# Identity products ahead of four waits of TensorE: at three stage ends and at the first gate item

## The chip, the cores and the metric

The kernel runs on one core of one Trainium2 chip. A core has five engines that run their own streams of instructions and meet at semaphores: TensorE (in the rows PE; its weight loads are PEld), VectorE (DVE), ScalarE (ACT), GpSimd (POOL) and SyncE (SP), which issues most of the DMAs. TensorE reads operands from SBUF and writes psum, eight banks of 2 KB per partition, 512 columns of fp32 each. TensorE's clock has two levels, 1.2 and 2.4 GHz; the profile shows the granted share of the full one as PEclk, 0.50 and 1.00. The metric is the device time of one execution in microseconds.

## The reference

Two transformer blocks, one after the other, on a sequence of 1024 tokens of width 1024, batch 1, in fp32. The first mixes a sliding-window attention (window 128, 8 heads, with sinks) and an mLSTM; the second mixes a retention and a sparse attention that picks, for each query, the highest-scored keys by an indexer. Each has a feed-forward part.

```python
def first_block(x, c, ...):
    shift_m, scale_m, gate_m, shift_f, scale_f, gate_f = jnp.split(c @ w_ada + b_ada, 6, axis=-1)
    h = modulate(rms_norm(x, g_pre_mix), shift_m, scale_m)
    q_a, k_a, v_a, q_m, k_m, v_m, o_m, i_m, f_m, g_a, g_m = jnp.split(h @ w_in, ...)
    # window attention y_a; conv, silu, mlstm_chunkwise, head_layer_norm -> y_m
    # sigmoid(g_a) * (y_a @ w_branch_attn) + sigmoid(g_m) * (y_m @ w_branch_mlstm), then @ w_out
    # x + gate * rms_norm(...); then gate/up/down feed-forward, x + gate * rms_norm(...)

def second_block(x, ...):
    rq, rk, rv, rg, aq, ak, av, iq, ik, iw = split_columns(rms_norm_2(h, mix_norm_pre) @ w_in)
    ret_out = retention(rope(rq), rope(rk), rv, rg)
    att_out = dsa_attention(rope(aq), rope(ak), av, rope(iq), rope(ik), iw)   # top-k keys per query
    h = h + rms_norm_2(concatenate([ret_out, att_out]) @ w_out, mix_norm_post)
    up = causal_dwconv(rms_norm_2(h, ffn_norm_pre) @ w_up, conv_w, conv_b)
    h = h + rms_norm_2((silu(g) * u) @ w_down, ffn_norm_post)

reference = second_block(first_block(x, ...), ...)
```

## The kernel before

Every large product is made in three parts to reach fp32's precision on a faster format: an operand x is split into a high part (rounded, made mostly by ACT) and a low part (the rest, made by POOL or DVE), and `multiply` (L132 to L136) issues high x high (L134), low x high (L135) and high x low (L136), 512 columns each.

The program is a row of stages, each a `with nc.Block()`, in which each engine has its own hand-written order: rows of the first block, window attention with the convolution, the recurrent stage, then (`scores_phase`) the output projection, the feed-forward part of the first block and the index scores of the second, then the spread stage (`spread_phase`), then (`close_last`) the second block's output projection and feed-forward part. A stage ends with a barrier of all five engines: each engine drains (a DRAIN on its queue) and signals, POOL collects the signals and releases all. Between the stages of this change `core.renew_sems` (L83 to L87) then clears the semaphores (POOL) and makes a second such barrier.

`recurrent_phase` (L1018): the mLSTM in chunks of 128 tokens, beside it 16 gate products; at its end TensorE runs, for 16 items i, `gate(M + i, 0, KD)` and `branches(i)`, the last of which VectorE merges into `mT` (L1338 to L1341). The next stage begins with `Closing.pe` (L2158), whose first products (L2136) wait for the first operand split by ACT (L2066) and DVE (L2075); its first weights, `w_hi`/`w_lo` or `next_hi`/`next_lo`, lie ready.

`scores_phase` (L2461) ends on TensorE with `unit(n)` (L2575): products of keys and index queries, which ACT passes through relu (L2790) and DVE adds up into `bias` (L2704), eight units to a tile of queries.

`spread_phase` (L3310): 40 items (c, t), five groups of 512 columns of `w_in_2` (Q_, K_, V_, G_ gates, A_ attention queries) by eight tiles of 128 tokens; the bank of an item is `bank(n)`, n % 3 up to the gates. The weights of a group come k by k: SP loads `raw`, ACT makes the high part (L3692), POOL the low one (L3651); the first two k of Q_ (`first_hi`, `first_lo`) lie ready. VectorE runs a bitwise search for the top-k threshold (L2926 to L2951) throughout, with the rope of an item (L3580 to L3583) or a step of the retention between its steps; ACT counts for it (L2940) and copies V_ items out of psum (L3749). `bank_free(n)` lets TensorE wait until the item three before has been read. At the first gate item (G_, 0), TensorE waits for the banks of items n and n + 1, turns the first keys (`ret.turn_keys`, L3016 to L3019) and then computes both items in turns (`pair`). The stage ends with the last values of the sparse attention (L3201), the transposes of the sums (L3220), and VectorE's last scaling.

`Closing.keep_warm` (L2182) is there before: products of the identity with itself, 128 columns into a bank that nobody reads. It is called with 6 at L2178 and with 5 at L1635, in the output projection of each block.

Of the kernel before, what the change touches and what calls it, by code (L numbers as in the profile page):

```python
# [13 lines left out]
P = 128  # L14
# [117 lines left out]
def multiply(nc, out, stationary, moving, start, stop):  # L132

    nc.tensor.matmul(out, stationary.hi, moving.hi, start=start, stop=False)  # L134
    nc.tensor.matmul(out, stationary.hi, moving.lo, start=False, stop=False)  # L135
    return nc.tensor.matmul(out, stationary.lo, moving.hi, start=False, stop=stop)  # L136
# [881 lines left out]
def recurrent_phase(core, at, h, wv, wba, wbm, qT, kT, v, R, gcol, dec, yaT, soT, w_norm, ya, ym, mT, spill, next_w, cst):  # L1018
# [31 lines left out]
    INTER, UPDATE, INTRA = (5, 6), (7, 4), (3, 2)  # L1050
    head_at = lambda banks, hd: core.ps[:, banks[hd // 2], hd % 2 * E:(hd % 2 + 1) * E]

    with nc.Block() as block:
# [80 lines left out]
        def _(pe):  # L1134
            def gate(s, first, last):
                T, hf = s // 2, s % 2
                if first == 0:
                    if hf == 0 and T:
                        pe.wait_ge(split_done, T)
                    if s >= 2:  # L1140
                        pe.wait_ge(sig_done, s - 1)
                for k in range(first, last):
                    done = multiply(nc, core.ps[:, hf, :], w[:, T % 2, k], h.half(k, hf), k == 0, k == KD - 1)
                if last == KD:
                    done.then_inc(mm_done, 1)
# [51 lines left out]
            def branches(i):  # L1197
                m, hf = i // 2, i % 2
                tok = slice(hf * HALF, (hf + 1) * HALF)
                if i == 0:  # L1200
                    pe.wait_ge(ya_lo, KB)
                    pe.wait_ge(ym_lo, KB)
                if hf == 0:
                    pe.wait_ge(wb_split, m + 1)
                if i >= 2:
                    pe.wait_ge(merged, i - 1)
                for b, y in enumerate((ya, ym)):
                    for k in range(KB):
                        last = multiply(nc, core.ps[:, 2 + 2 * hf + b, :], wb[:, b, k], y(k, tok), k == 0, k == KB - 1)
                last.then_inc(br_done, 1)  # L1210

            for st in range(STEPS):
                n = at_step(st, 0, EVERY, TB)
                if n is not None:
                    opening(n)
                n = at_step(st, EVERY // 2, EVERY, TB)
# [6 lines left out]
            for i in range(M):  # L1223
                gate(M + i, 0, KD)
                branches(i)

        @block.vector
        def _(dve):
# [732 lines left out]
        return 3 if conv else 2  # L1961


class Closing:


# [42 lines left out]
    def at_step(self, u):  # L2009

        return (u, u % 2 * 2) if u < self.kt else ((u - self.kt) % self.kt, (u - self.kt) % 4)
# [168 lines left out]
                self.turn(pe, 2 * (u - kt - 10) + 1)  # L2180

    def keep_warm(self, bank, many):  # L2182
        for _ in range(many):
            self.nc.tensor.matmul(self.core.ps[:, bank, 0:P], self.cst["ident"], self.cst["ident"], start=True, stop=True)

    def turn_bank(self, n):
        return 4 + n % 2 if n < KD else self.late_banks[n % len(self.late_banks)]
# [273 lines left out]
def scores_phase(core, stage, closing, h, wv, base, tables, tables_dram, cos, sin, cst, k_hi, k_lo, av, iw, bias, first_raw, first_w):  # L2461
# [23 lines left out]
    bank = lambda n: (0, 2, 1)[n % 3]  # L2485
# [16 lines left out]
    with nc.Block() as block:  # L2502
# [26 lines left out]
        def _(pe):  # L2529
# [21 lines left out]
            def left(what):  # L2551

                if what[0] == S_:
                    pe.wait_ge(keys_out, what[1] + 1)
                else:
                    pe.wait_ge(parts_out_done, parts_no[what] + 1)

            def turn(c, t, a=0):
                m = place[c, t, a]
                if m < 3:  # L2560
                    pe.wait_ge(closing.squared, closing.square_no(15))
                else:
                    left(turns[m - 3 if m < 12 else m - 1])
                at = turn_bank(m)
                if c == S_:
                    pe.wait_ge(rr_ready, number[c, t] + 1)
                    for j in range(2):
                        last = nc.tensor.transpose(core.ps[:, at, j * P:(j + 1) * P], rs[:, t % 2, j * P:(j + 1) * P], cst["ident"])
                else:
                    pe.wait_ge(q_lo, t - 1)  # L2570
                    for q in range(4):
                        last = nc.tensor.transpose(core.ps[:, at, q * P:(q + 1) * P], q_rows[:, 4 * a + q, :, :].bitcast(F32), cst["ident"])
                last.then_inc(turned, 1)
# [73 lines left out]
            for n in range(3 * RH, len(units)):  # L2647
                unit(n)
                if n - 3 * RH in (4, 7):
                    turn(I_, 7, (n - 3 * RH) // 6)  # L2650

        @block.vector
        def _(dve):
# [656 lines left out]
def spread_phase(core, h, wv, cos, sin, cst, bias, retention_of, spill, q_rows, q_tiles, tops, sparse_of, first_w, next_w, next_raw, next_first):  # L3310
# [12 lines left out]
    with ExitStack() as scope:  # L3323
# [6 lines left out]
        bank = lambda n: n % 3 if n < A_ * TB else n % 2  # L3330
# [41 lines left out]
        with nc.Block() as block:  # L3372
# [34 lines left out]
            def _(pe):  # L3407
# [58 lines left out]
                def turn_free(what):  # L3466
                    if place[what]:
                        pe.wait_ge(turn_out, place[what])
# [14 lines left out]
                for n, (c, t) in enumerate(items):  # L3483
                    if c == Q_ or t > 1 or (c, t) == (A_, 0):
                        bank_free(n)
                    elif t == 0:
                        bank_free(n)
                        if c == G_:
                            bank_free(n + 1)
                    if c == G_ and t == 0:  # L3490
                        turn_free((K_, 0))
                        ret.turn_keys(pe, 0).then_inc(turned, 1)
                        pair(n, 0, 4)
# [65 lines left out]
                for half in range(2):  # L3559
                    att.values(pe, TB * RH - 2, half)  # L3560
                att.turn_sums(pe, TB - 1)

            @block.vector
            def _(dve):
# [434 lines left out]
```

## Time and profile before

| | |
|---|---|
| time, median of 3 runs | 2876.22 us (2875.53 to 2876.64) |
| the profiled execution: its time | 2871.56 us |
| its span, first to last instruction | 2869.8 us |
| mean granted TensorE clock over the span | 0.984 |
| TensorE busy | 2753.2 us, 96%, 13656 products |
| VectorE busy | 1806.6 us, 63% |
| ACT, POOL busy | 1244.5 us, 43%; 1177.1 us, 41% |
| DMA | 272.35 MB, mean 95 GB/s |

A wait's releaser is the instruction whose semaphore came last. A product's row starts when it starts to stream; its duration holds the latency through the array, so that the rows of one stream overlap, and the distance of two starts is what one costs. Most large products run as one instruction each in the trace; a view of the trace counts instructions, the order counts products as the program issues them. A DRAIN stands on the engine's queue ("PEldq", "DVEq"); its start is when the queue reaches it and its duration how long it holds there.

### The profile page before, as it was taken

How to read it: one execution, taken by the hardware profiler on the slowest of the kernel's cores; microseconds unless marked ns; L12 is line 12 of the kernel's file. 1: busy time of each engine (PE TensorE's matmuls, PEld its weight loads, DVE VectorE, ACT ScalarE, POOL GpSimd, SP SyncE). 2: the span in 40 equal slices, each digit the busy share in tenths (PEclk: the TensorE clock that was granted, in tenths of full speed). 3: DMA queues.
4: the chain of work that ended last, by engine and by line, in shares of the span. 5: the costliest groups of instructions: out<-in, count | busy, mean ns of one | idle time of the engine just before them, and what ended most of it. 6: DMA issues, size and time to landing. Idle time of an engine off the chain costs nothing. (4 is left out here: it accounts for less than half of the span.)

```text
span 2869.8 us, 38822 instructions
## 1 busy us (share of the span) xinstructions
PE 2753.2 (96%) x13656; PEld 2260.2 (79%) x13656; DVE 1806.6 (63%) x2690; ACT 1244.5 (43%) x2267; POOL 1177.1 (41%) x826
## 2 busy tenths in 40 slices
PE   6999999999999999999999899989999999999998
PEld 6877788887788888888888677877778888887886
DVE  6758757323676666621845999785567778776153
ACT  6225545101533333323654677547453444443243
POOL 2011222333734444544641242521173466675454
PEclk8999999999999999999999999999999999999999
DMA  7431112323422222245530123100242222124452
GB/s 261 154 118 30 30 45 63 107 66 103 140 78 70 88 88 74 87 169 164 180 119 2 44 67 96 46 15 9 82 147 67 81 73 88 66 80 169 151 192 90
DMA packets 176237, 272.35 MB, mean 95 GB/s; under 512 B 13145, under 2 KB 105561, under 8 KB 176089
## 3 DMA queue, kind: packets, MB, share of 16 engines
q1 hardware_dynamic: 176088, 270.39, 28.6%
q8 instruction: 91, 1.49, 0.2%
q14 instruction: 58, 0.47, 0.1%
HBM read 224.21 MB, written 46.14 MB: 94 GB/s over the span
## 5 line engine op out<-in xcount | busy, mean ns | idle before, releaser
L2083 POOL TENSOR_TENSOR sb_out_lo<-sb_out_raw,sb_out_hi 128x512 fp32r<-128x512 f32 (+1 forms) x174 | 311.9, 1801 | 312.2 <-ACT sb_out_hi L2070 312.1
L134 PE MATMUL psum<-sb_out_hi,sb_a_hi 128*128 128x512 f32 x912 | 357.8, 392 | 5.7 <-ACT sb_junk L2294 4.4
L136 PE MATMUL psum<-sb_out_hi,sb_a_lo 128*128 128x512 f32 x912 | 355.1, 389 | 0.0
L135 PE MATMUL psum<-sb_out_lo,sb_a_hi 128*128 128x512 f32 x912 | 355.0, 389 | 0.0
L1556 POOL TENSOR_TENSOR sb_pair_lo<-sb_pair_sum,sb_pair_hi 128x512 fp32r<-128x512 f32 x180 | 236.7, 1326 | 269.7 <-ACT sb_pair_hi L1700 269.7
L134 PE MATMUL psum<-sb_h_hi,sb_w_hi 128*128 128x512 f32 x640 | 256.7, 401 | 2.9 <-DVE sb_h_lo L2230 2.4
L136 PE MATMUL psum<-sb_h_hi,sb_w_lo 128*128 128x512 f32 x640 | 249.6, 390 | 0.0
L135 PE MATMUL psum<-sb_h_lo,sb_w_hi 128*128 128x512 f32 x640 | 249.6, 390 | 0.0
L134 PE MATMUL psum<-sb_h_hi,sb_pair_hi 128*128 128x512 f32 x576 | 224.1, 389 | 0.0
L135 PE MATMUL psum<-sb_h_lo,sb_pair_hi 128*128 128x512 f32 x576 | 224.1, 389 | 0.0
L136 PE MATMUL psum<-sb_h_hi,sb_pair_lo 128*128 128x512 f32 x576 | 224.1, 389 | 0.0
L1700 ACT ACTIVATE sb_pair_hi<-sb_pair_sum 128x512 fp32r<-128x512 f32 x180 | 113.2, 630 | 237.6 <-DVE sb_pair_sum L1840 164.2
L134 PE MATMUL psum<-sb_w_hi,sb_h_hi 128*128 128x512 f32 (+1 forms) x496 | 197.4, 398 | 12.0 <-DVEq L3583 5.0
L134 PEld LDWEIGHTS psum<-sb_out_hi,sb_a_hi 128*128 128x128 f32 x912 | 171.2, 188 | 46.4 <-ACT sb_junk L2294 7.3
L136 PEld LDWEIGHTS psum<-sb_out_hi,sb_a_lo 128*128 128x128 f32 x912 | 171.2, 188 | 36.0
L135 PEld LDWEIGHTS psum<-sb_out_lo,sb_a_hi 128*128 128x128 f32 x912 | 171.3, 188 | 34.3
L1909 DVE TENSOR_TENSOR sb_gate_up<-sb_gate_up,psum 128x512 f32<-128x512 f32 x216 | 138.6, 682 | 86.0 <-PE psum L136 84.1
L136 PE MATMUL psum<-sb_w_hi,sb_h_lo 128*128 128x512 f32 (+1 forms) x496 | 190.7, 384 | 0.0
L135 PE MATMUL psum<-sb_w_lo,sb_h_hi 128*128 128x512 f32 (+1 forms) x496 | 190.6, 384 | 0.0
L134 PE MATMUL psum<-sb_h_sum_hi,sb_pair_hi 128*128 128x512 f32 x432 | 168.4, 390 | 1.8 <-ACT sb_gate_up L1760 1.2
L1840 DVE TENSOR_TENSOR sb_pair_sum<-sb_pairs_raw 128x512 f32<-128x512 f32 x144 | 161.8, 1144 | 10.6 <-POOL sb_pair_lo L1556 8.2
L135 PE MATMUL psum<-sb_h_sum_lo,sb_pair_hi 128*128 128x512 f32 x432 | 168.1, 389 | 0.0
(487 smaller groups left out, 6383.9 us busy)
## 6 DMA issues: line engine op xcount, KB each, us to landing
act_kept<-sb_gate_up SPq DMA_DIRECT2D x40, 512.0 KB, 2.8
sb_pairs_raw<-in_w_up SPq DMA_DIRECT2D x18, 1024.0 KB, 5.2
sb_late_w<-in_w_ada SPq DMA_DIRECT2D x32, 512.0 KB, 4.8
sb_w_raw<-in_w_in SPq DMA_DIRECT2D x54, 256.0 KB, 3.1
sb_out_raw<-in_w_ffn_down SPq DMA_DIRECT2D x44, 256.0 KB, 3.1
sb_out_raw<-in_w_down SPq DMA_DIRECT2D x44, 256.0 KB, 2.8
sb_act_ring<-act_kept SPq DMA_DIRECT2D x40, 256.0 KB, 4.0
sb_act_late<-act_kept SPq DMA_DIRECT2D x40, 256.0 KB, 4.0
```

The source lines that it names most:

```text
L134: nc.tensor.matmul(out, stationary.hi, moving.hi, start=start, stop=False)
L135: nc.tensor.matmul(out, stationary.hi, moving.lo, start=False, stop=False)
L136: return nc.tensor.matmul(out, stationary.lo, moving.hi, start=False, stop=stop)
L1556: self.nc.gpsimd.tensor_tensor(self.wp.lo[:, p], src, self.wp.hi[:, p].bitcast(F32), ALU.subtract).then_inc(self.pair_lo, 1)
L1700: self.nc.scalar.activation(self.wp.hi[:, p], src, ACT.Copy).then_inc(self.pair_hi, 1)
L1840: ops.tensor_tensor(t, a, b, op).then_inc(self.pair_sum if p < self.by_dve else self.pool_pair, 1)
L1909: nc.vector.tensor_tensor(dest, a, self.core.ps[:, bank, :], op).then_inc(self.part, 1)
L2083: self.nc.gpsimd.tensor_tensor(w.lo, raw, w.hi.bitcast(F32), ALU.subtract).then_inc(self.w_lo, 1)
```

## The change

A function `keep_warm(core, cst, pe, bank, many)` issues `many` products of the identity with itself, 128 columns each, into one bank; the method of `Closing` calls it now. Four calls are new. In `recurrent_phase` 36 products into bank 5 stand at the end of TensorE's program (site 1). In `scores_phase` 54 into bank 3 stand at its end (site 2). In `spread_phase` 22 into `bank(n)` stand at the first gate item behind its `bank_free` calls and ahead of `turn_free` (site 3), and 26 into bank 4 at the end (site 4). No other engine's instructions change.

```diff
@@ -1223,6 +1223,7 @@
             for i in range(M):
                 gate(M + i, 0, KD)
                 branches(i)
+            keep_warm(core, cst, pe, INTER[1], 36)
 
         @block.vector
         def _(dve):
@@ -1961,6 +1962,11 @@
         return 3 if conv else 2
 
 
+def keep_warm(core, cst, pe, bank, many):
+    for _ in range(many):
+        pe.matmul(core.ps[:, bank, 0:P], cst["ident"], cst["ident"], start=True, stop=True)
+
+
 class Closing:
 
 
@@ -2180,8 +2186,7 @@
                 self.turn(pe, 2 * (u - kt - 10) + 1)
 
     def keep_warm(self, bank, many):
-        for _ in range(many):
-            self.nc.tensor.matmul(self.core.ps[:, bank, 0:P], self.cst["ident"], self.cst["ident"], start=True, stop=True)
+        keep_warm(self.core, self.cst, self.nc.tensor, bank, many)
 
     def turn_bank(self, n):
         return 4 + n % 2 if n < KD else self.late_banks[n % len(self.late_banks)]
@@ -2648,6 +2653,7 @@
                 unit(n)
                 if n - 3 * RH in (4, 7):
                     turn(I_, 7, (n - 3 * RH) // 6)
+            keep_warm(core, cst, pe, 3, 54)
 
         @block.vector
         def _(dve):
@@ -3488,6 +3494,7 @@
                         if c == G_:
                             bank_free(n + 1)
                     if c == G_ and t == 0:
+                        keep_warm(core, cst, pe, bank(n), 22)
                         turn_free((K_, 0))
                         ret.turn_keys(pe, 0).then_inc(turned, 1)
                         pair(n, 0, 4)
@@ -3559,6 +3566,7 @@
                 for half in range(2):
                     att.values(pe, TB * RH - 2, half)
                 att.turn_sums(pe, TB - 1)
+                keep_warm(core, cst, pe, 4, 26)
 
             @block.vector
             def _(dve):
```

TensorE at the end of the recurrent stage, before: the last products of `branches` (`sb_ym` is the mLSTM's output, `sb_branch` the branch weight), the branch out of the block and into the next, the first products of the output projection. "waits" names the semaphores waited for; names are shared by semaphores of other stages.

```order
L136 MATMUL psum<-sb_ym_hi_3903,sb_branch_lo_3913 128x512
L134 MATMUL psum<-sb_ym_hi_3903,sb_branch_hi_3912 128x512
L135 MATMUL psum<-sb_ym_lo_3904,sb_branch_hi_3912 128x512
L136 MATMUL psum<-sb_ym_hi_3903,sb_branch_lo_3913 128x512
L1053 UNCONDITIONAL_BRANCH
L2528 UNCONDITIONAL_BRANCH [waits barrier_Pool_Activation_PE_DVE_SP_release]
L134 MATMUL psum<-sb_w_hi_82,sb_a_hi_6607 128x512 [waits y_ready_61,root_60]
```

The same place in the changed program:

```order
L136 MATMUL psum<-sb_ym_hi_3903,sb_branch_lo_3913 128x512
L134 MATMUL psum<-sb_ym_hi_3903,sb_branch_hi_3912 128x512
L135 MATMUL psum<-sb_ym_lo_3904,sb_branch_hi_3912 128x512
L136 MATMUL psum<-sb_ym_hi_3903,sb_branch_lo_3913 128x512
L1967 MATMUL psum<-sb_consts_49 128x128 x36
L1053 UNCONDITIONAL_BRANCH
L2533 UNCONDITIONAL_BRANCH [waits barrier_Pool_Activation_PE_DVE_SP_release]
L134 MATMUL psum<-sb_w_hi_82,sb_a_hi_6643 128x512 [waits y_ready_61,root_60]
```

The 36 products stand ahead of the branch with the barrier, behind all real work of the stage. Sites 2 and 4 read alike, with 54 and 26.

TensorE at the first gate item, before: the last products of the V_ group, the transposes of the first keys (L3019), the first gate product. `raw_got5_99` is the name under which the wait for ACT's reading of the bank appears.

```order
L134 MATMUL psum<-sb_w_hi_13493,sb_h_hi_14_62 128x512
L135 MATMUL psum<-sb_w_lo_13494,sb_h_hi_14_62 128x512
L136 MATMUL psum<-sb_w_hi_13493,sb_h_lo_15_63 128x512
L3019 MATMUL psum<-sb_consts_49,sb_k_rows_13463 128x128 [waits hi_done_102,x_got5_41,raw_got5_99]
L3019 MATMUL psum<-sb_consts_49,sb_k_rows_13463 128x128 x3
L134 MATMUL psum<-sb_w_hi_13493,sb_h_hi_12_60 128x512 [waits raw_got1_95]
L135 MATMUL psum<-sb_w_lo_13494,sb_h_hi_12_60 128x512
```

The same place in the changed program, where the transposes' line is L3025:

```order
L134 MATMUL psum<-sb_w_hi_13583,sb_h_hi_14_62 128x512
L135 MATMUL psum<-sb_w_lo_13584,sb_h_hi_14_62 128x512
L136 MATMUL psum<-sb_w_hi_13583,sb_h_lo_15_63 128x512
L1967 MATMUL psum<-sb_consts_49 128x128 [waits raw_got5_99]
L1967 MATMUL psum<-sb_consts_49 128x128 x21
L3025 MATMUL psum<-sb_consts_49,sb_k_rows_13553 128x128 [waits x_got5_41,hi_done_102]
L3025 MATMUL psum<-sb_consts_49,sb_k_rows_13553 128x128 x3
L134 MATMUL psum<-sb_w_hi_13583,sb_h_hi_12_60 128x512 [waits raw_got1_95]
```

The wait for ACT's reading moved from the transposes to the first identity product.

For the counts, the old call with 6 products in the program before (`sb_consts` holds the identity), among the products of the output projection and the transposes of L2196:

```order
L134 MATMUL psum<-sb_out_hi_6605,sb_a_hi_6607 128x512
L135 MATMUL psum<-sb_out_lo_6606,sb_a_hi_6607 128x512
L136 MATMUL psum<-sb_out_hi_6605,sb_a_lo_6608 128x512
L2184 MATMUL psum<-sb_consts_49 128x128 x6
L2196 MATMUL psum<-sb_consts_49,sb_rows_mid_6603 128x128 [waits late_got0_76]
L2196 MATMUL psum<-sb_consts_49,sb_rows_mid_6603 128x128 x7
L134 MATMUL psum<-sb_out_hi_6605,sb_a_hi_6607 128x512 [waits y_ready_61,root_60]
```

Nothing moves here; in the profile this line has 44 instructions for the two calls of each block, 6 and 5 products.

## Rows read from the trace of the kernel before

**Rows 1.** all waits of TensorE: line, releaser, us in total, times, longest
```profile
PE psum L134 <- DVE sb_a_lo L2075: 10.0, 3, 5.2
PE psum L134 <- POOLq L3654: 7.7, 1, 7.7
```

**Rows 2.** windows: length, busy us and counts by engine, PEclk, DMA share, GB/s
```profile
46.30:49.20 2.90, 2.82 (x13) 2.52 (x12) 2.21 (x6) 2.08 (x4) 0.00 (x0) 0.50 0.98 372
...
692.90:699.60 6.70, 4.11 (x10) 3.28 (x11) 2.86 (x10) 2.72 (x4) 0.78 (x1) 0.50 0.68 212
...
1616.00:1766.00 150.00, 142.86 (x608) 113.44 (x608) 140.04 (x377) 108.30 (x214) 49.94 (x38) 0.97 0.25 78
...
1768.10:1774.80 6.70, 5.13 (x14) 3.89 (x15) 6.60 (x8) 5.55 (x11) 5.27 (x4) 0.50 0.37 89
...
1788.60:1795.30 6.70, 6.70 (x40) 6.47 (x38) 4.74 (x14) 1.70 (x4) 1.75 (x2) 0.50 0.09 28
...
2061.70:2064.90 3.20, 3.20 (x9) 2.46 (x8) 1.63 (x7) 1.58 (x2) 0.61 (x1) 0.50 1.07 346
```

**Rows 3.** timeline of TensorE, site 1: start, us, instruction, [idle before <-releaser]
```profile
689.95 0.39 PE L136 MATMUL psum<-sb_ym_hi,sb_branch_lo 128*128 128x512 f32 x1
695.49 0.80 PE L134 MATMUL psum<-sb_w_hi,sb_a_hi 128*128 128x512 f32 x1 [5.15 <-DVE sb_a_lo L2075]
...
697.36 0.63 PE L135 MATMUL psum<-sb_w_lo,sb_a_hi 128*128 128x512 f32 x1
697.78 0.63 PE L136 MATMUL psum<-sb_w_hi,sb_a_lo 128*128 128x512 f32 x1
...
699.81 0.39 PE L135 MATMUL psum<-sb_w_lo,sb_a_hi 128*128 128x512 f32 x1
700.04 0.39 PE L136 MATMUL psum<-sb_w_hi,sb_a_lo 128*128 128x512 f32 x1
```

**Rows 4.** line of the barrier ending the recurrent stage: took min/median/max ns, start
```profile
L1053 PEldq DRAIN  x1: 4267/4267/4267, 686.1 to 686.1; - x1
L1053 DVEq DRAIN  x1: 725/725/725, 691.8 to 691.8; - x1
```

**Rows 5.** timeline of TensorE: groups of 128-column products
```profile
46.21 2.91 PE L239 MATMUL psum<-sb_consts 128*128 128x128 f32 x12
...
776.52 1.50 PE L2184 MATMUL psum<-sb_consts 128*128 128x128 f32 x12
...
2186.72 1.28 PE L2184 MATMUL psum<-sb_consts 128*128 128x128 f32 x10
```

**Rows 6.** line of the barrier that ends the spread stage
```profile
L3372 DVEq DRAIN  x1: 698/698/698, 2058.0 to 2058.0; - x1
```

**Rows 7.** timeline of TensorE, site 4
```profile
2056.62 0.66 PE L3220 MATMUL psum<-sb_consts,sb_inverse_sums 128*128 128x128 f32 x4
2061.22 0.50 PE L134 MATMUL psum<-sb_next_hi,sb_a_hi 128*128 128x512 f32 x1 [3.95 <-DVE sb_a_lo L2075]
```

**Rows 8.** line of the barrier that ends the scores stage
```profile
L2502 DVEq DRAIN  x1: 17/17/17, 1614.0 to 1614.0; - x1
```

**Rows 9.** timelines of TensorE and POOL, site 2 and the stage behind it
```profile
1607.60 0.39 PE L2587 MATMUL psum<-sb_ik_lo,sb_iq_tile 128*128 128x512 f32 x1
...
1621.18 0.52 PE L134 MATMUL psum<-sb_w_hi,sb_h_hi 128*128 128x512 f32 x1
...
1619.83 7.54 POOL L3651 TENSOR_TENSOR sb_w_lo<-sb_w_raw,sb_w_hi 128x512 fp32r<-128x512 f32 x6 [31.20 <-ACT sb_w_hi L3692]
...
1720.10 0.69 PE L134 MATMUL psum<-sb_w_hi,sb_h_hi 128*128 128x512 f32 x1 [3.05 <-DVEq L3583]
```

**Rows 10.** timeline of TensorE, site 3 and the next meeting with VectorE
```profile
1768.65 1.09 PE L3019 MATMUL psum<-sb_consts,sb_k_rows 128*128 128x128 f32 x4 [3.72 <-ACT sb_rotated L3749]
1770.76 0.80 PE L134 MATMUL psum<-sb_w_hi,sb_h_hi 128*128 128x512 f32 x1 [1.02 <-POOL sb_w_lo L3651]
...
1788.28 0.60 PE L3044 MATMUL psum<-sb_state,sb_q_decayed 128*128 128x128 f32 x2 [1.90 <-DVE sb_scores L3098]
```

## The prediction

> **What bounds the kernel now.** I read the page first: TensorE (PE in the rows) is busy 96% of a span of 2869.8 us. What is left to win on it are 117 us of idle time and the stretches in which its products ran slowly. Then I read the list of its waits, sorted by length, and the timelines around the longest. Four are the places of this change: 5.2 us at the end of the recurrent stage (site 1), 7.7 us at the end of the scores stage (site 2), 3.7 us at the first gate item (site 3) and 3.95 us at the end of the spread stage (site 4) [rows 1, 7, 10]. Behind sites 1, 3 and 4 TensorE resumes at 1.2 GHz: the windows show a granted clock of 0.50 [rows 2]. At that level 512 columns cost 0.43 us, at 2.4 GHz 0.23 us [rows 3]. After site 1 ten products run so, 10 x 0.20 = 2.0 us lost; after site 4 a little over 3.2 us do, half of it lost, 1.7 us [rows 2].
>
> Then I asked who ends each wait. Sites 1, 2 and 4 are ends of a stage, and a stage ends with a barrier of all engines. The view of the barrier's line shows a DRAIN on each engine's queue. TensorE's at site 1 starts at 686.1 and holds for 4.27 us, until 690.37, right when its last product ends (689.95 + 0.39) [rows 3, 4]. So a DRAIN waits for the products ahead of it. VectorE's ends last, at 691.8 + 0.73 = 692.53 [rows 4]. TensorE's slack at site 1 is therefore 692.53 - 690.37 = 2.2 us, not 5.15. The other 695.49 - 692.53 = 2.96 us lie behind the DRAINs (the release, a second barrier, ACT's and VectorE's split of the first operand), and no work ahead of the barrier can lie beside them.
>
> **What an added product costs.** The call exists already with 6 products and with 5, as the order shows. The timeline has them as 12 and as 10 instructions: an fp32 product that is no transpose runs as two. They take 1.50 and 1.28 us, so one more product costs 0.22 us [rows 5]. That makes 1.50 + 30 x 0.22 = 8.1 us for 36, 12.1 us for 54, 5.0 us for 22 and 5.9 us for 26, all at full clock. This step carries the whole forecast: reading the rows as one instruction per product gives half. At half clock the nearest row is six such products at 46.21: 2.91 us, 0.485 us each, at a clock of 0.50 [rows 2, 5].
>
> *The Trainium skill ("TensorE: Matmul & The Clock Gate", section "Back-to-back issue gap") gives some 81 ns for each product of 128 columns in a stream. By that 36 would take 2.9 us and 26 would take 2.1 us, the DRAINs of sites 1 and 4 would end some 0.6 and 0.5 us behind VectorE's and that of site 2 before it, a sum of about +1. The page's figure is not for fp32; the rows are of this very call, read 0.22 us, and decide.*
>
> **Site 1, 36 products.** They start one slot behind the last real one, at 690.18, and end at 698.3. TensorE's DRAIN then ends 698.3 - 692.53 = 5.8 us behind VectorE's. All engines wait for it, and so do the loads of the next stage, which are issued behind the barrier: **+5.8 us**, with nothing to hide it.
>
> **Site 2, 54 products.** From one slot behind the last real product, 1607.83, until 1619.9. VectorE's DRAIN, the last one, ended at 1614.0 + 0.02 [rows 8, 9]. **+5.9 us**. VectorE's top-k search, which fills the next stage, starts that much later: it is busy 140.04 of the first 150 us there [rows 2] and cannot catch up.
>
> **Site 4, 26 products.** The four transposes before them start at 2056.62 and take four slots of 0.11 us, so they run from 2057.06 until 2063.0; VectorE's DRAIN ended at 2058.0 + 0.70 = 2058.70 [rows 6, 7]. **+4.3 us**.
>
> **What the clock gives back.** Behind the barriers TensorE idles as before: 2.96 us at site 1, 2061.22 - 2058.70 = 2.52 us at site 4, 1.7 us at site 2 (1607.60 + 0.39 + 7.7 = 1615.7, less 1614.02) [rows 1, 8, 9]. In this trace the clock fell around a wait of 3.05 us (the product at 1720.10 reads 0.69 us, one behind a wait at full clock 0.52) and around one of 1.90 us that had small products before it (0.50 for the 6.7 us behind 1788.6) [rows 2, 9, 10]. The new idle times lie between, with dense work ahead of them. I take half of what there is to win: -1.0 of 2.0 us at site 1, **-0.8** of 1.7 at site 4, with bounds of nothing and all. At site 2 a full clock buys nothing: the first twelve products use weights that lie ready, the next need one that loads, ACT and POOL make behind the barrier. POOL makes six in 7.54 us from 1619.83, the first by 1621.1, and TensorE, at half clock, takes it at 1621.18 [rows 9]. Twelve faster products only lengthen that wait by 2.4 us.
>
> **Site 3, 22 products.** The order shows that they don't stand where the words say. The long wait (3.72 us, ended by ACT's copy L3749) is for a free bank; the products stand behind it, so that wait is now on the first of them, and they run when the real work is ready. Before, four transposes at 1768.65 took 1.09 us and TensorE then idled 1.02 us for POOL's first weight [rows 10]. That is the cover. The clock was at half from 1768.1 on [rows 2]; with dense products I let half clock last some 3.4 us, as behind 2061.7, so 5.0 us of products become 6.7. The first gate product comes 6.7 - 1.0 = 5.7 us late less 0.5 for faster transposes; its nine slow successors [rows 2] are then fast, 1.8 us. That is 3.4 us late. The next meeting with VectorE is at 1788.28, where TensorE waited 1.90 us [rows 10]: 1.5 us are left. With no such wait the clock may hold behind it, which spares up to half of 6.7 us. Bounds: -2 us if it does, and 22 x 0.485 - 1.0 - 1.9 = +7.8 us if all run at half clock. I take **+1.0**, near the row of 2061.7.
>
> **Sum.** 5.8 + 5.9 + 4.3 - 1.0 - 0.8 + 1.0 = **+15.2 us** on the profiled execution of 2871.56 us. It was 4.66 us faster than the median of the three timed runs; the terms are barriers that every run has, so they are added to the median: 2876.22 + 15.2 = **2891.4 us**, +0.53%. What lies within 0.2%, 5.75 us (2870.5 to 2882.0), counts as the same, since a measurement of this kernel can tell about that much from no change.
>
> **The rivals.**
> - *The forecast*, 0.56: 2891.4, by itself 2888.5 to 2894.5.
> - *B, the clock holds everywhere*, 0.18: dense identity products keep it at 2.4 GHz over all the idle times. 16.0 - 2.0 - 1.7 and site 3 at -2 to +1: +10.3 to +13.3, 2888. *The Trainium skill's rule ("TensorE: Matmul & The Clock Gate", "Why this matters for your kernels") is to leave no long idle gaps between bursts, so that the rate doesn't drop; by that rule B comes.* Against it stands the fall around 1.90 us.
> - *E, the gate item at half clock*, 0.14: the 22 products never get the full clock, and the delay reaches ACT's copy of the turned keys and so VectorE: 16.0 - 1.8 + 7.8 = +22: 2898.2.
> - *C, no slower: TensorE's DRAIN doesn't hold the others*, 0.06: they pass the barrier at their old times and only TensorE is late. It is 698.3 - 695.49 = 2.8 us late at site 1 and 1.8 at site 4, less the clock's 2.0 and 1.7; at site 2 it comes at 1619.9, its twelve products end 1.5 us behind POOL's weight, which VectorE's search hides. With site 3 that is +1.9: 2878.1, the same. Against it: the DRAIN's end at 690.37.
> - *D, one instruction per product in this build*, 0.04: 4.1, 6.1, 2.6 and 3.0 us. Sites 1 and 4 move by 1.8 and 1.4, site 2 by nothing, less 1.8 for the clock: +1.4, 2877.6; with all of the clock and of site 3, 2870, faster. It needs half of the rows' counts.
> - *F, the clock falls within the identity products*, 0.02: 2905.
>
> Range: D and C left out below, F above: 2887.0 to 2899.0. Chances: slower 0.90; same 0.09 (C, most of D); faster 0.01.
>
> **What would show it.** 72, 108, 44 and 52 instructions on the new line, 0.11 us apart. TensorE's DRAIN is the last at the three barriers, 5.8, 5.9 and 4.3 us behind VectorE's; the first product follows 2.96, 1.70 and 2.52 us behind it. If the clock behind sites 1 and 4 reads 1.00, B is right; if VectorE's DRAIN is still the last and the others pass, C. At site 3 the first identity product starts with the end of ACT's copy. The forecast is wrong if the three DRAINs are not late by 16 us together, or if the spread stage from barrier to barrier grows by other than 4.3 us and -2 to +3.

## The result, and the profile after

The changed kernel takes 2885.62 us (median of 7 runs, 2883.26 to 2886.55), the kernel before in the same comparison 2875.53 us (7 runs, 2871.66 to 2876.74). The ratio is 1.0038, with an interval of 1.0027 to 1.0050: **10.1 us slower**. The sign of the forecast and its largest part, the late barriers, are right; the time lies below its range (2887.0 to 2899.0) and 5.8 us below the forecast. A later comparison of the same two kernels (below, e11_after) gave 1.0043 (1.0029 to 1.0057), and all runs of this study together have medians of 2873.35 us before (111 runs, 2863.34 to 2880.21) and 2885.3 us after (14 runs): +12.0 us.

The profiled execution of the changed kernel has a span of 2883.8 us and 13932 products on TensorE where the one of before has 13656: 276 more, two for each of the 138 added. The first view is the lines of the three barriers (minimum/median/maximum ns, start), VectorE's and TensorE's DRAIN of each; they answer to [rows 4, 6, 8].

```profile
L1053 DVEq DRAIN  x1: 725/725/725, 695.6 to 695.6; - x1
L1053 PEldq DRAIN  x1: 2173/2173/2173, 700.1 to 700.1; - x1
...
L2507 DVEq DRAIN  x1: 17/17/17, 1619.2 to 1619.2; - x1
L2507 PEldq DRAIN  x1: 2173/2173/2173, 1623.0 to 1623.0; - x1
...
L3378 DVEq DRAIN  x1: 698/698/698, 2068.0 to 2068.0; - x1
L3378 PEldq DRAIN  x1: 2173/2173/2173, 2070.9 to 2070.9; - x1
```

TensorE's DRAIN now ends last each time: at 702.27 against VectorE's 696.33, at 1625.17 against 1619.22, at 2073.07 against 2068.70. That is 5.9, 6.0 and 4.4 us, 16.3 together; the forecast had 5.8, 5.9 and 4.3.

The waits of TensorE (line, releaser, us in total, times, longest) show the other side, to be read against [rows 1]:

```profile
PE psum L134 <- DVE sb_a_lo L2081: 6.4, 3, 3.0
...
PE psum L1967 <- ACT sb_rotated L3757: 3.8, 1, 3.8
```

The idle time at site 1 is 3.0 instead of 5.2 us. The one at site 3 is as long as before and now ends on the first identity product: the products stand behind it. In the list the kernel looks better than before, and it is slower: what left this list went into the DRAINs, which the list doesn't show.

Windows of the changed kernel (length, busy us and counts of PE, PEld, DVE, ACT and POOL, PEclk, DMA share, GB/s), at the places of [rows 2]:

```profile
705.80:709.20 3.40, 3.40 (x9) 2.64 (x8) 1.53 (x6) 1.58 (x2) 0.53 (x1) 0.50 1.06 345
2075.50:2078.70 3.20, 3.15 (x14) 2.60 (x15) 2.17 (x9) 1.01 (x2) 0.00 (x0) 1.00 1.03 330
1787.00:1793.80 6.80, 6.80 (x42) 5.35 (x41) 6.63 (x11) 5.86 (x12) 5.44 (x4) 1.00 0.60 185
```

Behind site 1 the clock was at half for 3.4 us; before it had been so for 6.8 us, of which 4.2 lay behind the first product (695.49 to 699.7). Behind site 4 it held; behind the gate item it was full. The barriers' 16.3 us stand against a span that grew by 14.0 us, but the two traced executions differ by 3.8 us ahead of site 1 already, where the programs are the same. One pair of traces therefore doesn't tell where the rest went. The experiments give the stages of 18 executions.

### The profile page after: what moved, and what is told of

Same layout as the page of the kernel before. It is cut to its first block and busy times, and to the rows that moved or that the text cites. A ratio compares the mean times of both kernels' runs of the same rounds, so it can differ in the third digit from the quotient of the medians.

```text
span 2883.8 us, 39374 instructions
## 1 busy us (share of the span) xinstructions
PE 2779.0 (96%) x13932; PEld 2286.8 (79%) x13932; DVE 1804.0 (63%) x2690; ACT 1244.6 (43%) x2267; POOL 1178.9 (41%) x826
## 5 line engine op out<-in xcount | busy, mean ns | idle before, releaser
L134 PE MATMUL psum<-sb_w_hi,sb_h_hi 128*128 128x512 f32 (+1 forms) x496 | 196.9, 397 | 12.9 <-DVEq L3591 5.0
```

## The experiments

Each stage is measured from the end of the last DRAIN of one barrier to the end of VectorE's DRAIN at the next; "late" is how far the last DRAIN ends behind VectorE's. All in us, one traced execution a row. The expectations end the last stage at VectorE's last DRAIN instead, 3.0 us earlier (808.1 us for the 811.1 of the first row).

| execution | start to site 1 | late | site 1 to 2 | late | site 2 to 4 | late | site 4 to the end | span |
|---|---|---|---|---|---|---|---|---|
| before | 692.5 | 0 | 921.5 | 0 | 444.7 | 0 | 811.1 | 2869.8 |
| before (e0) | 695.4 | 0 | 918.4 | 0 | 442.4 | 0 | 810.5 | 2866.7 |
| before (e12) | 691.7 | 0 | 918.5 | 0 | 446.0 | 0 | 810.6 | 2866.8 |
| before (e13) | 696.6 | 0 | 920.3 | 0 | 449.3 | 0 | 812.2 | 2878.4 |
| after | 696.3 | 5.9 | 916.9 | 6.0 | 443.5 | 4.4 | 810.7 | 2883.8 |
| after (e11) | 695.2 | 5.8 | 916.7 | 6.0 | 443.3 | 4.4 | 812.5 | 2884.0 |
| after (e14) | 693.5 | 5.8 | 915.6 | 5.9 | 445.1 | 4.4 | 811.7 | 2882.1 |
| after (e15) | 696.0 | 5.9 | 915.6 | 6.0 | 443.1 | 4.4 | 812.1 | 2883.2 |
| e1, site 1 alone | 692.5 | 5.9 | 915.9 | 0 | 441.9 | 0 | 811.0 | 2867.3 |
| e2, site 2 alone | 694.0 | 0 | 917.9 | 6.0 | 443.0 | 0 | 811.6 | 2872.5 |
| e3, site 3 alone | 695.1 | 0 | 918.6 | 0 | 443.0 | 0 | 812.0 | 2868.7 |
| e4, site 4 alone | 694.1 | 0 | 917.8 | 0 | 445.2 | 4.4 | 809.5 | 2871.0 |
| e5, behind the barriers | 695.0 | 0 | 919.3 | 0 | 441.9 | 0 | 810.2 | 2866.4 |
| e6, within the slack | 697.4 | 0 | 920.5 | 0 | 445.8 | 0 | 810.5 | 2874.2 |
| e7, ahead and behind | 694.1 | 0 | 916.4 | 0 | 441.8 | 0 | 809.2 | 2861.5 |
| e8, 72 at site 1 | 696.4 | 13.9 | 919.6 | 6.0 | 446.2 | 4.4 | 808.9 | 2895.5 |
| e9, e7 with site 3 | 697.9 | 0 | 917.0 | 0 | 445.4 | 0 | 808.4 | 2868.7 |
| e10, e9 with 26 at site 2 | 695.2 | 0 | 918.0 | 0.3 | 443.5 | 0 | 809.8 | 2866.8 |

The late columns repeat within 0.1 us. Everything else moves by several us between executions of one kernel.

**One place at a time.** Of the four new calls three are left out; e1 keeps the first, e2 the second, e3 the third, e4 the last:

```diff
+            keep_warm(core, cst, pe, INTER[1], 36)
+            keep_warm(core, cst, pe, 3, 54)
+                        keep_warm(core, cst, pe, bank(n), 22)
+                keep_warm(core, cst, pe, 4, 26)
```

> Only the 36 products ahead of the barrier behind the recurrent stage; the other three places as before. Theory A (each place costs what its DRAIN comes late, and the clock gives back only what runs at half rate right behind it): TensorE's DRAIN at that barrier ends 5.8 to 5.9 us behind VectorE's, the stretch from that barrier to the one behind the scores stage is 0 to 2 us shorter, the whole is +4 to +6 us. Rival B (the products change the clock far behind the barrier as well, which gives the 4.6 us that the next stage was shorter in the changed kernel): the same 5.9 us at the barrier, but the stretch behind it is 4 to 5 us shorter, the whole +1 to +2 us. Rival N (the 4.6 us are chance: half-rate stretches that come and go in code the change doesn't touch): the stretch behind it differs from before's by -5 to +1 us in a way that kernels without these products show as well.

> Only the 54 products ahead of the barrier behind the scores stage. Theory A: TensorE's DRAIN ends 5.9 us behind VectorE's, the spread stage keeps its length within 0.5 us, the whole is +5.9 us. Rival B: the clock holds at the start of the spread stage and the stage is 1 us or more shorter, +4.9 us or less. Rival N: the time ahead of this barrier differs from before's by several us, though nothing there is changed.

> Only the 22 products at the first gate item. Theory A (as forecast): the spread stage from barrier to barrier is 1.0 us longer, with bounds of -2 and +7.8, the whole +1 us. Rival B: by the difference of the two traces (the spread stage was 1.15 us shorter with sites 2 and 3 together, from release to VectorE's DRAIN) these products win 1.2 us, the whole -1.2 us. Rival N: what lies ahead of the stage moves the whole by more than this.

> Only the 26 products ahead of the barrier behind the spread stage. Theory A: TensorE's DRAIN ends 4.3 to 4.4 us behind VectorE's; behind it half of 1.7 us is won, +3.5 us. Rival B: the clock reads 1.00 from the first product behind the barrier on, all of 1.7 us is won, +2.6 us. The changed kernel's trace had the clock at 1.00 there, but its last stages were only 0.4 us shorter, so A and B differ by what else moves there.

| kept | median us (before 2872.22) | ratio | interval | in us | forecast |
|---|---|---|---|---|---|
| site 1 | 2875.42 | 1.0012 | 1.0003 to 1.0021 | +3.4 | +4.8 |
| site 2 | 2879.36 | 1.0024 | 1.0015 to 1.0033 | +6.9 | +5.9 |
| site 3 | 2870.53 | 0.9998 | 0.9989 to 1.0007 | -0.6 | +1.0 |
| site 4 | 2875.80 | 1.0006 | 0.9997 to 1.0016 | +1.7 | +3.5 |

The column in us is the ratio times 2872; the medians themselves differ by +3.2, +7.1, -1.7 and +3.6 us, and each interval reaches some 2.6 us to either side. The four ratios add up to +11.4 us, 1.0040, and the change as a whole gave 1.0038 and 1.0043: within this noise the places add up. Site 1's +3.4 lies between theory A (+4 to +6) and B (+1 to +2), site 2's fits A, and sites 3 and 4 don't tell A from B. In e1 the clock never fell behind site 1 (the same columns of windows):

```profile
701.40:708.20 6.80, 6.76 (x38) 5.88 (x39) 2.70 (x10) 1.97 (x3) 3.34 (x2) 1.00 0.93 300
```

The stage behind it was short, 915.9 us, as rival B had it. But e2, e3 and e4, which have nothing at site 1, took 917.8 to 918.6 us and not the 921.5 of the first trace: a part of what looked like a gain was that trace. So N holds for a part of it, and how much is left for B one execution of e1 can't tell.

**Products where nobody waits for them.** e5 has none of the four calls and six products as the first work of the stages behind sites 1 and 4; e6 has only as many products as end before VectorE's DRAIN; e7 joins the two without site 2; e0 is the kernel before once more.

```diff
 class Closing:
     def pe(self, pe):
         kt, nc = self.kt, self.nc
+        if not self.before:
+            self.keep_warm(0, 6)
...
+            keep_warm(core, cst, pe, INTER[1], 9)
...
+                keep_warm(core, cst, pe, 4, 6)
```

e5 is the first hunk, e6 the other two and 26 products at site 2, e7 all that is shown.

> None of the four places. Instead six identity products behind the barriers of sites 1 and 4, as the first work of TensorE in the next stage (bank 0, which the stage's first product writes anew). Six take 1.3 us at full clock; the barrier's release came some 1.5 us behind the last DRAIN and the first product 2.96 us behind it, so they should end before its operand is there. Theory A (the clock is all that identity products can win, and they cost only where a DRAIN waits for them): no barrier later, the stage behind site 1 up to 2.0 us shorter than the 917.8 to 918.6 us that it took in the kernels without products there, the last stage up to 1.7 us shorter than 808.1 to 809.0; the whole -1 to -3.5 us. Rival B (the products must stand ahead of the idle time to hold the clock): both stages as before, the whole within 0.5 us of before.

> Products ahead of the barriers only as many as end before VectorE's DRAIN: 9 at site 1 (2.0 us in a slack of 2.15), 26 at site 2 (5.7 in 5.9), 6 at site 4 (1.3 in 1.34 to 1.44), none at site 3. Theory A: VectorE's DRAIN stays the last or TensorE's is late by 0.2 us at most, so the cost of +16.3 us is gone. What the clock gives depends on the idle time that is left, 3.0, 2.0 and 2.5 us as in the changed kernel: where it held there it holds here, -1.6 us behind site 1 and -1.0 behind site 4, the whole -3 us, 0.9990. Rival B (it takes the long run of products to hold the clock): 0 to -1 us.

> 9 products ahead of the barrier of site 1 and 6 ahead of that of site 4, and six behind each; sites 2 and 3 without. Theory A: no barrier late, TensorE never idle for more than some 2 us around either, clock 1.00 behind both, -2.0 and -1.7 us, the whole -3 to -3.7 us. Rival B (the clock falls all the same, or the six behind the barrier run at half clock, 0.485 us each, and delay the first product by 1.5 us): 0 to +3 us.

> The kernel before once more, for the length of its stages in a second traced execution. Theory N (4 us and more of the difference between the two traced executions came from code that the change doesn't touch): the stage between sites 1 and 2 takes 917.8 to 918.6 us, as in the three kernels without products at site 1, not the 921.5 of the first trace, and the way to site 1 692.5 to 694.5. Rival: 921.5 again, then the three others were shortened by something in them.

Measured, against a median of 2873.90 us of before: e5 2868.93 us, 0.9989 (0.9980 to 0.9998); e6 2872.78 us, 0.9996 (0.9987 to 1.0004); e7 2864.73 us, **0.9974 (0.9965 to 0.9983)**; e0 0.9999 (0.9990 to 1.0009). e5 gained what theory A allowed. e6 did not reach A's -3 us: the clock fell behind both of its barriers. e0 took 918.4 us between sites 1 and 2, as theory N said.

The timeline of TensorE in e5, where the six stand behind 3.76 us of idle time, and that of e7, where nine more stand ahead of it (start, us, instruction, [idle before <-releaser]):

```profile
696.63 2.58 PE L1966 MATMUL psum<-sb_consts 128*128 128x128 f32 x12 [3.76 <-PEq L86]
698.87 0.77 PE L134 MATMUL psum<-sb_w_hi,sb_a_hi 128*128 128x512 f32 x1
```

```profile
691.79 2.17 PE L1967 MATMUL psum<-sb_consts 128*128 128x128 f32 x18
695.71 1.57 PE L1967 MATMUL psum<-sb_consts 128*128 128x128 f32 x12 [1.75 <-PEq L86]
697.09 0.50 PE L134 MATMUL psum<-sb_w_hi,sb_a_hi 128*128 128x512 f32 x1
```

In e5 the clock has fallen, the six take 2.58 us instead of some 1.5, and the first real product comes 3.85 us behind the barrier instead of 2.97: behind a long idle time they are late themselves. (At site 4 of e5 the six stand behind 2.56 us of idle time; there they took 1.58 us and the clock held.) In e7 the idle time is cut into pieces of less than 2 us, the six run at full clock, and the first real product comes 2.97 us behind the barrier, as before. The windows of e7 behind sites 1 and 4 read full clock from the first product on:

```profile
697.10:703.90 6.80, 6.80 (x40) 5.96 (x39) 2.74 (x10) 2.64 (x3) 3.53 (x3) 1.00 1.00 298
2054.70:2058.00 3.30, 3.30 (x17) 2.77 (x16) 2.15 (x9) 1.30 (x2) 0.16 (x1) 1.00 1.02 328
```

Its barriers aren't late (TensorE's DRAIN at 691.8 + 2.17, VectorE's at 693.4 + 0.72). The gain, 7.5 us by the ratio and 4.9 at the interval's near end, is larger than the 3.7 us that theory A could pay for. Part of the rest has rows. The old identity products behind each barrier ([rows 5], 776.52 and 2186.72) serve as marks; in e7 they are at 776.17 and 2178.63:

```profile
776.17 1.50 PE L1967 MATMUL psum<-sb_consts 128*128 128x128 f32 x12
2178.63 1.28 PE L1967 MATMUL psum<-sb_consts 128*128 128x128 f32 x10
```

That is 82.05 and 126.3 us behind the barriers; the seven executions with nothing at site 1, and the seven with nothing at site 4, took 84.5 and 128.5 us on average. So 2.5 and 2.2 us, 4.7 together, lie right behind the two barriers. The stretch near 1502 us that e7 lacks (below) is worth 1.0 to 3.3 us where it comes; what is left has no row. The two DRAINs of e7 at site 1:

```profile
L1053 PEldq DRAIN  x1: 2168/2168/2168, 691.8 to 691.8; - x1
L1053 DVEq DRAIN  x1: 723/723/723, 693.4 to 693.4; - x1
```

**More and fewer.** e8 is the changed kernel with 72 for 36 at site 1. e9 is e7 with site 3's call, e10 is e9 with `keep_warm(core, cst, pe, 3, 26)` at site 2. e11 is the changed kernel again.

> The changed kernel with 72 products instead of 36 at site 1. Theory A (each product holds the barrier 0.22 us, one for one): TensorE's DRAIN ends 5.95 + 36 x 0.22 = 13.9 us behind VectorE's, the whole is 7.9 us slower than the changed kernel, 1.0038 + 0.0028 = 1.0066 of before. Rival C (a late DRAIN is partly made up for behind the barrier): less than 1.0055.

> The changed kernel once more, timed and traced beside the others. The four places alone gave 1.0012, 1.0024, 0.9998 and 1.0006, a sum of +0.40%: theory A (the places add up) expects 1.0040 within 0.001, the DRAINs late by 5.9, 5.9 and 4.4 us again, 916 to 917 us between sites 1 and 2 and 806.5 to 807.8 in the last stage. Rival N (the first comparison, +10.1 us, was low because its executions fell well): 1.0050 or more.

> 9 and 6 products ahead of the barriers of sites 1 and 4, six behind each, and the 22 at the gate item; none at site 2. Theory A (site 3 is worth -1.5 us where the clock would have fallen behind it and +0.7 us where it would not): the whole -7 us again, 0.9974 within 0.001, with site 3 giving nothing a measurement can tell. Rival (the 22 products win by themselves): 0.9965 or less.

> As the last one, with 26 products at site 2 as well, which end before VectorE's DRAIN. Theory A (at site 2 a full clock buys nothing, since POOL's weight and VectorE's search come later anyway): the same as without them, 0.9974 within 0.001. Rival: they hold the clock in the spread stage's first items and give 1 to 2 us more.

Measured, against 2873.07 us: e8 2892.39 us, 1.0061 (1.0046 to 1.0077, 4 runs); e11 2885.85 us, 1.0043 (1.0029 to 1.0057); e9 2868.84 us, 0.9981 (0.9972 to 0.9990); e10 2868.83 us, 0.9987 (0.9978 to 0.9996). TensorE's DRAIN in e8, to be read against VectorE's end at 696.4:

```profile
L1053 PEldq DRAIN  x1: 2173/2173/2173, 708.2 to 708.2; - x1
```

It ends at 710.37, 13.9 us late: (13.94 - 5.94) / 36 = **0.222 us** for one more product, all of it on the path. e8's total can't tell theory A (1.0066) from rival C (1.0055). e11 came as theory A had it in total and in the DRAINs; its last stage, 809.5 us to VectorE's DRAIN, was longer than A's 806.5 to 807.8. e9 and e10 confirm that short runs of products make the kernel faster than before, and that site 3 and 26 products at site 2 add nothing that shows. In e9 as in e7 and e10 the clock read 1.00 for the first 6.8 us behind both barriers. e10's 0.9987 lies outside the 0.9974 within 0.001 that was expected; e7's 0.9974 is the lowest of the three and its interval overlaps with both; 0.998 is a fairer value for the group.

In e11 the clock fell behind sites 1 and 4 as it had in the kernel before, with idle times of 3.0 and 2.5 us as in the first trace of the changed kernel, where it held at site 4:

```profile
703.10:709.80 6.70, 5.74 (x14) 4.54 (x15) 2.86 (x10) 2.28 (x4) 2.29 (x1) 0.50 0.96 290
2075.30:2078.50 3.20, 3.20 (x9) 2.49 (x8) 0.72 (x2) 1.58 (x2) 1.31 (x1) 0.50 1.04 336
```

**What comes and goes.** Two further executions of each kernel, for the stages alone:

> One more traced execution of the kernel before, for its stages. Theory N (the stage between sites 1 and 2 varies by itself, by a half-rate stretch near 1502 us that comes and goes): 918 or 921 us. Theory B' (without products at site 1 that stretch comes in every second execution, with them never, and this is the part of the gain that the forecast lacked): 921 us in about half of such executions. The last stage 807.6 to 809.0.

> A further traced execution of the kernel before, with the same expectations: 918 or 921 us between sites 1 and 2 by theory N, 921 in about half of such executions by theory B'; the last stage 807.6 to 809.0.

> One more traced execution of the changed kernel. Theory N: between sites 1 and 2 about 917 us, in some executions 920, with the half-rate stretch near 1512 us (1502 plus the delay) in some. Theory B': never that stretch, 916 to 917.5 us. DRAINs late by 5.9, 5.9 and 4.4 us in every execution; the last stage 806 to 809.5.

> A further traced execution of the changed kernel, with the same expectations: by theory N the stretch near 1512 us in some executions, by theory B' in none; DRAINs late by 5.9, 5.9 and 4.4 us.

They took 2868.57 and 2880.21 us (before) and 2883.95 and 2885.05 us (after). The slowest, e13, shows what the fast ones lack. Windows of e13 and, below, the same ones of e0, at two places where TensorE has only short waits and small products:

```profile
1504.40:1511.20 6.80, 6.80 (x34) 6.64 (x32) 1.01 (x4) 1.74 (x4) 2.62 (x4) 0.50 0.01 2
1791.20:1804.80 13.60, 12.90 (x69) 11.19 (x69) 10.18 (x26) 5.41 (x11) 5.13 (x5) 0.50 0.12 39
```

```profile
1504.40:1511.20 6.80, 6.80 (x62) 6.80 (x63) 3.02 (x10) 2.71 (x9) 2.18 (x3) 1.00 0.01 2
1791.20:1804.80 13.60, 11.97 (x104) 9.96 (x101) 12.12 (x32) 9.75 (x21) 9.11 (x9) 1.00 0.25 79
```

The same program ran there at half clock in one execution and at full clock in the other: 34 product instructions against 62 in 6.8 us (e13 is 1.2 us behind e0 at the first place and 3.1 at the second). Over the 18 executions:

- **Near 1502 us** the stretch stands in 4 of the 9 that have nothing at site 1, or six products behind it or nine ahead of it alone (it is in before, e13, e5 and e6), and in 0 of the 9 others. It costs 1.0 to 3.3 us. But this grouping was made after the counts were seen. By the words of B', products at site 1 or none, the stretch stands in 2 of 7 without and, with e5 (six behind the barrier) and e6 (nine ahead), in 2 of 11 with them. So "with them never" does not hold for nine; for 36 and more it is 0 of 6 against 2 of 7, too few to tell B' from N.
- **Near 1788 us**, behind site 3, it stands in 5 of the 10 without site 3's call (before, e12, e13, e4, e6; spread stage 446.2 us on average) and not in the other 5 (442.2 us); in 0 of the 8 with it (444.1 us). These averages hold other stretches too. Closer in, between the two VectorE operations that start at 1779.31 and 1823.87 in the first trace, it took 44.4 to 47.2 us in the five with the stretch (45.5 on average), 42.0 to 42.3 (42.2) in the five without it, and 43.0 to 43.4 (43.3) in the eight with the 22 products. They cost 1.1 us where the clock would have held and save 2.2 us where it would have fallen, 0.6 us on average.
- **Near 1391 us** TensorE waits for VectorE's scaling of a row: 1.5 to 1.6 us in the first trace and in ten others, 0.5 us in e0, e12 and e13, and in none of the four traces of the changed kernel. Timeline rows of TensorE and of VectorE, kernel before, first trace:

```profile
1392.66 1.09 PE L2196 MATMUL psum<-sb_consts,sb_rows 128*128 128x128 f32 x8 [1.55 <-DVE sb_rows L2216]
...
1389.15 3.45 DVE L2216 TENSOR_SCALAR sb_rows<-sb_rows,sb_sums 128x1024 f32<-128x1024 f32 x2
```

and of VectorE in the changed kernel:

```profile
1397.66 2.45 DVE L2221 TENSOR_SCALAR sb_rows<-sb_rows,sb_sums 128x1024 f32<-128x1024 f32 x2
```

and of VectorE in e0, the pair ahead of it and this one:

```profile
1387.53 2.45 DVE L2216 TENSOR_SCALAR sb_rows<-sb_rows,sb_sums 128x1024 f32<-128x1024 f32 x2
1391.60 3.48 DVE L2216 TENSOR_SCALAR sb_rows<-sb_rows,sb_sums 128x1024 f32<-128x1024 f32 x2
```

A pair takes 2.45 us when one of its two operations takes 0.74 instead of 1.75 us. With neither pair short TensorE waits 1.5 us, with the first short 0.5, with both short not at all; this holds in all 18 executions. And a long operation is one that starts while POOL is busy: of the 360 scalings of this line in the 18 traces 169 are long, and at the start of 167 of these a POOL operation was running; at the start of the 191 short ones none was. So it is no effect of the clock, but of where POOL's and VectorE's operations fall against each other. Both pairs are short in the changed kernel in four executions of four, yet e1 (site 1 alone) and e8 (all four places) have the wait of 1.5 us: whether the change brings this about or it only happens to fit stays open.

## Why the forecast was right in its mechanism and missed its range

**The step that failed** is the sum of the small terms beside the barriers. Site 3 was put at +1.0 us and measured -0.6, and what happens away from the four places was put at nothing: in the traces of the changed kernel the stage behind site 1 lacks 2.5 us that no term had, 1.0 near 1391 us and 1.5 near 1502. That the change causes these 2.5 us is not shown. The rest of the miss lies in the baseline and in the range.

**The barriers: right.** This was the step that carried the forecast, two instructions and 0.22 us for each product, and a DRAIN that holds all engines. 5.8, 5.9 and 4.3 us were forecast; 5.9, 6.0 and 4.4 were measured, within 0.1 us in every execution, and 0.222 us a product in e8. Rivals C and D are refuted by the DRAINs and by the count of 276. *The Trainium skill's 81 ns for a product of 128 columns in a stream ("TensorE: Matmul & The Clock Gate", "Back-to-back issue gap") does not hold for this fp32 product: 222 ns were measured.* The words of the change name the right idle times, and yet the last 2.2, 6.0 and 1.4 us ahead of VectorE's DRAIN were the only room there, for 9, some 25 and 6 products: 26 at site 2 ended 0.3 us ahead of VectorE's DRAIN in e6 and 0.3 us behind it in e10.

**What the clock gives back right behind the barriers: right in size.** From site 1's barrier to the existing six products ([rows 5], 776.52, so 692.53 + 84.0; in the changed kernel 785.96, so 702.27 + 83.7) the seven executions with none at site 1 took 84.5 us on average, the six with 36 or 72 took 83.8: -0.7 us, forecast -1.0. Behind site 4 the six executions with 26 products took 810.9 us to the end, the seven with none there 811.3: -0.4, forecast -0.8; up to the five products at 2186.72 it was 127.2 against 128.5, -1.3. "Half of what there is to win" had the right reason at site 4: with 26 products the clock held there in three executions (the first trace, e4, e8) and fell in three (e11, e14, e15). At site 1 it fell in five of six, for 3.4 us in three and 6.8 us in two, and held in e1 alone. Where it held, the marks came 82.1 us (e1) and 126.4 to 126.5 us behind the barriers, 2.4 and 2.1 us early: all of what was to win, and a little more than the 2.0 and 1.7 of the forecast.

**Site 2: right.** +6.9 us alone (4.3 to 9.5), forecast +5.9. In the changed kernel its first products run at full clock and TensorE then waits 1.6 us for POOL's first weight, where the first trace of before had no such wait (e0 has one of 1.4); 26 products more or less (e9, e10) change nothing that shows.

**Site 3: the term was mis-sized.** Forecast +1.0, measured -0.6 alone (-3.2 to +2.0, which by itself would still allow +1.0) and -0.6 by the 18 traces, from the two VectorE operations named above. The cost was seen rightly: the 22 products take 6.8 us where 6.7 were forecast, partly at half clock, so that rival E, half clock for all of them, did not come. They delay the gate products, and the meeting at 1788.28 with its 1.90 us of idle time is gone. What was underpriced is the other side, "the clock may hold behind it": it holds in 8 of 8, and without the 22 it falls in every second execution, for 6.8 to 13.7 us there. Against the executions where it did not fall by itself +1.1 us were measured, near the forecast's +1.0. The row of the 22 products in the changed kernel:

```profile
1779.85 6.78 PE L1967 MATMUL psum<-sb_consts 128*128 128x128 f32 x44 [3.78 <-ACT sb_rotated L3757]
```

**Stretches far from the four places: missing in the sum.** The sum followed each product to the next wait and no further. The four traces of before and of the changed kernel differ on average by +1.2 (ahead of site 1, chance), +16.2 (late), -3.4 (site 1 to 2), -1.8 (site 2 to 4) and +0.7 us (the rest): +12.9. Of the -3.4, -0.6 lies right behind the barrier, -1.0 around the wait near 1391 us, -1.5 the stretch near 1502 us, -0.3 what follows. Two of these had no term. That the stretch near 1502 us goes away because of the products at site 1 is not shown; e1 lacks the stretch and still has the wait near 1391. Of the -1.8, -1.5 lies at the gate item: the clock fell behind it in three of the four traces of before, where five in ten did over all.

**The baseline: a part of the miss.** The forecast was added to 2876.22 us, a median of three runs within 1.1 us of each other, although the profiled execution beside it had taken 2871.56. The text noted the 4.66 us and let it be. 111 runs spread over 17 us around 2873.35. Of the 5.8 us between forecast and result, 0.7 lie in the baseline of the first comparison and 5.1 in the difference; against all runs of the study the miss is 6.1, 2.9 in the baseline and 3.2 in the difference (12.0 measured, 15.2 forecast).

**The range: too narrow below.** Rival B's own bounds reached down to +10.3 us, and the range was cut at 2887.0, inside B, as if the baseline were exact. The result is where B's time was, but not by B's mechanism: the clock held behind site 1 in one execution of six and behind site 4 in three. That the two times meet is luck. The Trainium skill's rule ("TensorE: Matmul & The Clock Gate", "Why this matters for your kernels"), to leave no long idle gaps between bursts, fits e7, e9 and e10, where no gap around the barriers is longer than 1.8 us and the windows read 1.00 behind both; e11 shows that a dense run ahead of one gap of 2.5 us doesn't do it by itself.

## What to carry to other kernels

Ahead of a barrier of all engines, the wait that an engine's list shows is not the room that it has: read the DRAINs, and fill only up to the end of the last one. To hold the clock over such a barrier, split the filling: as many small products as fit ahead of it, and a few as the first work behind it, so that no single idle time stays long. With both the clock held behind both barriers in three kernels of three (e7, e9, e10); products only ahead (e6) held it behind neither, products only behind (e5) behind one; here that turned 0.4% slower into 0.2% faster. A difference below 0.5% needs several traces of each kernel before a stage's change is read as an effect, and a baseline of more than three runs.

## What the runs showed of the hardware that was not expected

- The same program at the same place ran at 2.4 GHz in one execution and at 1.2 GHz in another, with idle times equal to 0.1 us: with 26 products ahead of 2.5 us of idle time the clock held in three executions of six, with 36 or 72 ahead of 3.0 us in one of six. In e13 TensorE's waits from 1480 to 1504.4 us, ahead of the first stretch, were 0.7 us in all, the longest 0.4.
- Six fp32 identity products behind 3.76 us of idle time took 2.58 us, and behind 1.75 us, with nine ahead, 1.57 us. Behind the long idle time they delayed the first real product by 0.9 us, and yet the time from the barrier to the existing six products was 83.7 us, against 84.5.
- A VectorE operation on 128 x 1024 fp32 (L2216) took 1.75 us when a POOL operation was running at its start and 0.74 us when none was, in 358 of 360 cases; two such took 2.45 or 3.45 us by where POOL's fell.
